# Weights of a two-layer hybrid model laid out contiguously, one 8 KB piece for each partition

## The reference, cut to what matters

```
h = x                                             # 256 tokens x 1024, float32
h = h + swa_sink_attention(rms_norm(h), a_w_qkv, a_b_qkv, a_sinks, a_w_o)
h = h + swiglu(rms_norm(h), f_w_gate, f_w_up, f_w_down)           # 1024 x 3584
h = h + gated_deltanet(rms_norm(h), b_w_in, b_conv_w, ..., b_w_o) # b_w_in 1024 x 4112
h = h + moe_swiglu(rms_norm(h), m_w_router, m_w_gate, m_w_up, m_w_down)  # 8 experts, top 2
return rms_norm(h)

def swiglu(h, w_gate, w_up, w_down):
    return (silu(h @ w_gate) * (h @ w_up)) @ w_down
```

## Time and profile before

| | |
|---|---|
| median of 3 runs | 1816.75 us (1814.03 to 1817.48) |
| span of the profiled execution | 1815.9 us, 0.85 below the median of the runs |
| TensorE busy | 1656.2 us, 91% |
| VectorE, ScalarE busy | 1285.9 us (71%), 1010.4 us (56%) |
| read from HBM | 431.73 MB, 238 GB/s over the span |
| mean granted clock of TensorE | 0.937 |

### The profile page before, as it was taken

One profiled execution on the slowest core, in us unless ns is written; L12 is line 12 of the kernel. 1 busy time (PEld: TensorE's weight loads), 2 busy tenths in 40 slices (PEclk: granted clock), 3 DMA queues, 4 the chain that ended last, 5 costly groups with the idle time before them and its releaser, 6 DMA issues.

```text
span 1815.9 us, 22294 instructions
## 1 busy us (share of the span) xinstructions
PE 1656.2 (91%) x8075; PEld 1380.0 (76%) x8075; DVE 1285.9 (71%) x1111; ACT 1010.4 (56%) x979; POOL 44.8 (2%) x42
## 2 busy tenths in 40 slices
PE   5889999979948587889999999999999999999996
PEld 4677888869838474778878878788788788788785
DVE  5735555548462433478898888888888888988885
ACT  3444334335421112267777767777777777777674
POOL 0000000000022020000000000000000000000000
PEclk9889999989968685889999999999999999999998
DMA  9214555535300000359999899899899899899992
GB/s 339 93 47 162 186 185 184 188 120 181 117 0 1 0 1 29 111 196 375 354 325 373 319 340 375 306 366 377 298 370 369 304 373 355 315 366 335 346 371 92
DMA packets 187186, 433.29 MB, mean 239 GB/s; under 512 B 9232, under 2 KB 9616, under 8 KB 187024
## 3 DMA queue, kind: packets, MB, share of 16 engines
q1 hardware_dynamic: 184032, 431.25, 66.1%
q10 hardware_dynamic: 3120, 1.56, 0.3%
HBM read 431.73 MB, written 1.05 MB: 238 GB/s over the span
## 4 chain that ended last, share of the span: by engine, by line
PE 81%; DVE 8%; ACT 6%; issue 3%; ACTq 1%; POOL 1%; DVEq 1%; POOLq 0%
PE PS L264 23%; PE PS L266 23%; PE PS L265 23%; ACT w_high L252 2%; DVE w_low L256 2%; PE PS L972 1%; PE PS L897 1%; PE PS L926 1%; PE PS L956 1%; PE PS L665 1%; PE PS L955 1%; PE PS L888 1%; PE PS L896 1%; ACT x_high L597 1%; PE PS L925 1%
## 5 line engine op out<-in xcount | busy, mean ns | idle before, releaser
L256 DVE TENSOR_TENSOR w_low<-w_raw,w_high 128x2048 fp32r<-128x2048 f32 x408 | 931.0, 2290 | 205.4 <-ACT w_high L252 203.4
L252 ACT ACTIVATE w_high<-w_raw 128x2048 fp32r<-128x2048 f32 x408 | 780.5, 1918 | 379.7 <-PE PS L266 378.7
L264 PE MATMUL PS<-w_high,x_high 128*128 128x512 f32 x1264 | 504.1, 399 | 23.1 <-DVE w_low L256 11.9
L266 PE MATMUL PS<-w_high,x_low 128*128 128x512 f32 x1264 | 495.2, 392 | 0.0
L265 PE MATMUL PS<-w_low,x_high 128*128 128x512 f32 x1264 | 494.9, 392 | 0.0
L264 PEld LDWEIGHTS PS<-w_high,x_high 128*128 128x128 f32 x1264 | 239.0, 189 | 82.1 <-DVE w_low L256 28.2
L266 PEld LDWEIGHTS PS<-w_high,x_low 128*128 128x128 f32 x1264 | 238.5, 189 | 51.2
L265 PEld LDWEIGHTS PS<-w_low,x_high 128*128 128x128 f32 x1264 | 238.9, 189 | 47.6
L264 PE MATMUL PS<-w_high,m_act_high 128*128 128x512 f32 x448 | 177.8, 397 | 0.0
L265 PE MATMUL PS<-w_low,m_act_high 128*128 128x512 f32 x448 | 177.3, 396 | 0.0
L266 PE MATMUL PS<-w_high,m_act_low 128*128 128x512 f32 x448 | 177.3, 396 | 0.0
(11 more groups left out here) (245 smaller groups left out, 1626.8 us busy)
## 6 DMA issues: line engine op xcount, KB each, us to landing
w_raw<-in_m_w_gate SPq DMA_DIRECT2D x112, 1024.0 KB, 6.9
w_raw<-in_m_w_up SPq DMA_DIRECT2D x112, 1024.0 KB, 6.9
w_raw<-in_m_w_down SPq DMA_DIRECT2D x112, 1024.0 KB, 6.4
w_raw<-in_b_w_in SPq DMA_DIRECT2D x16, 1024.0 KB, 5.5
w_raw<-in_f_w_gate SPq DMA_DIRECT2D x14, 1024.0 KB, 5.1
w_raw<-in_f_w_up SPq DMA_DIRECT2D x14, 1024.0 KB, 5.1
w_raw<-in_f_w_down SPq DMA_DIRECT2D x14, 1024.0 KB, 4.9
w_raw<-in_a_w_qkv SPq DMA_DIRECT2D x6, 1024.0 KB, 15.9
```

What stands on the lines that cost most here:

```text
L252: nc.scalar.activation(WH[:, n % SPLIT, :], W[:, n % RAW, :], ACT.Copy).then_inc(hi_done, 1)
L256: nc.vector.tensor_tensor(WL[:, n % SPLIT, :], W[:, n % RAW, :], WH[:, n % SPLIT, :].bitcast(f32), ALU.subtract).then_inc(lo_done, 1)
L264: nc.tensor.matmul(o, sH, mH, start=first, stop=False)
L266: return nc.tensor.matmul(o, sL, mH, start=False, stop=last)
```

## The change

The host cuts all large weights into blocks in the order in which SyncE reads them, each stored as 128 rows of 8 KB, one for each partition. Four arrays `w_att`, `w_ffn`, `w_gdn` and `w_moe` take the place of nine weight inputs, and `b_w_small` is the 16 columns of `b_w_in` that `small_w` takes. Every block then is one contiguous 1 MB in HBM. Slots, waits, order and the rest of the kernel stay as they are.

```diff
-        def fetch(sp, n, r, kind, src):
+        def fetch(sp, n, r, src):
             if n >= RAW:
                 sp.wait_ge(lo_done, n - RAW + 1 + r * RAW)
-            sp.dma_start(raw_view(n % RAW, kind), src).then_inc(w_in[n % RAW], 16)
+            sp.dma_start(W[:, n % RAW, :], src).then_inc(w_in[n % RAW], 16)
...
-        def col_src(w, cb, half):
-            return w.rearrange("(k p) c -> p k c", p=128)[:, 4 * half:4 * half + 4, cb * CH:(cb + 1) * CH]
...
+            def fetch_packed(n, w, first, last):
+                for i in range(first, last):
+                    fetch(sp, n + i, 0, w[i])
+
+            def ffn_stream(n0, r0, w, loop_r):
+
+                for i in range(4):
+                    fetch(sp, n0 + i, r0, w[i])
                 with sp.Fori(0, NC - 1) as i:
                     r = loop_r(i)
-                    for k, (w, half) in enumerate(((g, 0), (g, 1), (u, 0), (u, 1))):
-                        fetch(sp, n0 + 4 + k, r, "cols", block_of(w, half, i + 1))
-                    for half in range(2):
-                        fetch(sp, n0 + 8 + half, r, "rows", d[:, ds(4 * i + 2 * half, 2), :])
+                    for k in range(6):
+                        fetch(sp, n0 + 4 + k, r, w[ds(6 * i + 4 + k, 1)].rearrange("a p c -> p (a c)"))
...
             if "att" in stages:
-                fetch_cols(base["att"], a_w_qkv[0], 2)
+                fetch_packed(base["att"], w_att, 0, 4)
                 sp.dma_start(cst[:, 128:], consts[:, 128:]).then_inc(sem("cst_in"), 16)
-                fetch(sp, base["att"] + 4, 0, "cols", col_src(a_w_qkv[0], 2, 0))
-                fetch(sp, base["att"] + 5, 0, "cols", col_src(a_w_qkv[0], 2, 1))
-                fetch_cols(base["att"] + 6, a_w_o[0], D // CH)
+                fetch_packed(base["att"], w_att, 4, 10)
...
-                             (small_w[:, :, 0:16], b_w_in[0].rearrange("(k p) c -> p k c", p=128)[:, :, 4096:4112]),
+                             (small_w[:, :, 0:16], b_w_small.rearrange("(k p) c -> p k c", p=128)),
...
+def column_blocks(w):
+    n = w.shape[0]
+    c = w.shape[2] // CH
+    v = w.reshape(n, 2, 4, 128, c, CH).transpose(0, 4, 1, 3, 2, 5)
+    return v.reshape(n, c, 2, 128, SUB)
+
+
+def row_blocks(w):
+    n = w.shape[0]
+    return w.reshape(n, NC, 2, 2, 128, D).transpose(0, 1, 2, 4, 3, 5).reshape(n, NC, 2, 128, SUB)
```

More of the change, by code:

```diff
@@ L75, in constants, with hybrid_kernel @@
     return c
-def hybrid_kernel(nc, x, a_norm, a_w_qkv, a_b_qkv, a_sinks, a_w_o, f_norm, f_w_gate, f_w_up, f_w_down,
-                  b_norm, b_w_in, b_conv_w, b_a_log, b_dt_bias, b_o_norm, b_w_o,
-                  m_norm, m_w_router, m_w_gate, m_w_up, m_w_down, final_norm, consts, out,
+def hybrid_kernel(nc, x, a_norm, a_b_qkv, a_sinks, f_norm, b_norm, b_w_small, b_conv_w, b_a_log, b_dt_bias,
+                  b_o_norm, m_norm, m_w_router, final_norm, w_att, w_ffn, w_gdn, w_moe, consts, out,
                   stages=("att", "ffn", "gdn", "moe")):
@@ L275, in _ @@
         def _(sp):
-            def fetch_cols(n, w, blocks):
-                for cb in range(blocks):
-                    for half in range(2):
[L279 to L294, removed]
+            def fetch_packed(n, w, first, last):
[4 more added lines that the diff above has]
+                    fetch(sp, n0 + i, r0, w[i])
                 with sp.Fori(0, NC - 1) as i:
                     r = loop_r(i)
-                    for k, (w, half) in enumerate(((g, 0), (g, 1), (u, 0), (u, 1))):
-                        fetch(sp, n0 + 4 + k, r, "cols", block_of(w, half, i + 1))
-                    for half in range(2):
-                        fetch(sp, n0 + 8 + half, r, "rows", d[:, ds(4 * i + 2 * half, 2), :])
+                    for k in range(6):
+                        fetch(sp, n0 + 4 + k, r, w[ds(6 * i + 4 + k, 1)].rearrange("a p c -> p (a c)"))
                 for half in range(2):
-                    fetch(sp, n0 + SUBS_FFN - 2 + half, r0, "rows", d[:, 4 * (NC - 1) + 2 * half:4 * (NC - 1) + 2 * half + 2, :])
+                    fetch(sp, n0 + SUBS_FFN - 2 + half, r0, w[SUBS_FFN - 2 + half])
             x_v = x[0].rearrange("(t p) d -> p t d", p=128)
@@ L308, in _ @@
             if "att" in stages:
-                fetch_cols(base["att"], a_w_qkv[0], 2)
+                fetch_packed(base["att"], w_att, 0, 4)
                 sp.dma_start(cst[:, 128:], consts[:, 128:]).then_inc(sem("cst_in"), 16)
-                fetch(sp, base["att"] + 4, 0, "cols", col_src(a_w_qkv[0], 2, 0))
-                fetch(sp, base["att"] + 5, 0, "cols", col_src(a_w_qkv[0], 2, 1))
-                fetch_cols(base["att"] + 6, a_w_o[0], D // CH)
+                fetch_packed(base["att"], w_att, 4, 10)
             if "ffn" in stages:
-                ffn_stream(base["ffn"], 0, f_w_gate, f_w_up, f_w_down, lambda i: i)
+                ffn_stream(base["ffn"], 0, w_ffn, lambda i: i)
             if "gdn" in stages:
-                fetch_cols(base["gdn"], b_w_in[0], 8)
-                fetch_cols(base["gdn"] + 16, b_w_o[0], D // CH)
+                fetch_packed(base["gdn"], w_gdn, 0, 20)
             if "moe" in stages:
                 def job(j, e):
-                    ffn_stream(base["moe"], j * NC, m_w_gate[0, ds(e, 1)], m_w_up[0, ds(e, 1)], m_w_down[0, ds(e, 1)],
-                               lambda i: j * NC + i)
+                    n0, r0 = base["moe"], j * NC
+                    w = w_moe[ds(e, 1)].rearrange("a n p c -> (a n) p c")
+                    for i in range(4):
+                        fetch(sp, n0 + i, r0, w[i])
+                    with sp.Fori(0, NC - 1) as i:
+                        for k in range(6):
+                            fetch(sp, n0 + 4 + k, r0 + i, w[ds(6 * i + 4 + k, 1)].rearrange("a p c -> p (a c)"))
+                    for half in range(2):
+                        fetch(sp, n0 + SUBS_FFN - 2 + half, r0, w[SUBS_FFN - 2 + half])
                 with sp.Fori(0, E) as j:
@@ L1527, in _, with ffn_order @@
                                        op0=ALU.mult, op1=ALU.mult).then_inc(sem("fin_done"), 1)
-_INS = ['x', 'a_norm', 'a_w_qkv', 'a_b_qkv', 'a_sinks', 'a_w_o', 'f_norm', 'f_w_gate', 'f_w_up', 'f_w_down',
-        'b_norm', 'b_w_in', 'b_conv_w', 'b_a_log', 'b_dt_bias', 'b_o_norm', 'b_w_o',
-        'm_norm', 'm_w_router', 'm_w_gate', 'm_w_up', 'm_w_down', 'final_norm']
+_INS = ['x', 'a_norm', 'a_b_qkv', 'a_sinks', 'f_norm', 'b_norm', 'b_w_small', 'b_conv_w', 'b_a_log', 'b_dt_bias',
+        'b_o_norm', 'm_norm', 'm_w_router', 'final_norm', 'w_att', 'w_ffn', 'w_gdn', 'w_moe']
+def column_blocks(w):
[6 more added lines that the diff above has]
+    return w.reshape(n, NC, 2, 2, 128, D).transpose(0, 1, 2, 4, 3, 5).reshape(n, NC, 2, 128, SUB)
+def ffn_order(gate, up, down):
+    g, u, d = column_blocks(gate), column_blocks(up), row_blocks(down)
+    out = np.empty((gate.shape[0], SUBS_FFN, 128, SUB), np.float32)
+    out[:, 0:2], out[:, 2:4] = g[:, 0], u[:, 0]
+    for i in range(NC - 1):
+        n = 4 + 6 * i
+        out[:, n:n + 2], out[:, n + 2:n + 4], out[:, n + 4:n + 6] = g[:, i + 1], u[:, i + 1], d[:, i]
+    out[:, SUBS_FFN - 2:] = d[:, NC - 1]
+    return out
 def kernel(**inputs):
@@ L1539, with blocks @@
     nc = _bacc.Bacc("TRN2", target_bir_lowering=False, num_devices=1)
+    laid = {k: np.asarray(v) for k, v in inputs.items()}
+    def blocks(name, columns):
+        return column_blocks(laid[name][:, :, 0:columns]).reshape(-1, 128, SUB)
+    laid["w_att"] = np.concatenate([blocks("a_w_qkv", QKV), blocks("a_w_o", D)])
+    laid["w_gdn"] = np.concatenate([blocks("b_w_in", 4 * D), blocks("b_w_o", D)])
+    laid["b_w_small"] = laid["b_w_in"][0, :, 4 * D:]
+    laid["w_ffn"] = ffn_order(laid["f_w_gate"], laid["f_w_up"], laid["f_w_down"])[0]
+    laid["w_moe"] = ffn_order(laid["m_w_gate"][0], laid["m_w_up"][0], laid["m_w_down"][0])
     arrays, args = {}, []
     for name in _INS:
-        a = np.ascontiguousarray(inputs[name])
+        a = np.ascontiguousarray(laid[name])
         arrays[f"in_{name}"] = a
```

## The result

The changed kernel takes 1829.3 us in the median of four runs (1828.5 to 1830.0); the kernel before, run beside it, 1816.3. The ratio is 1.0072, 95% interval 1.0058 to 1.0087: slower by 0.7%. The profiled execution has a span of 1827.8 us, 11.9 more than before, and its own time is 1829.57.

The account below looks back on a forecast made before the run. TensorE was taken to bound the expert jobs, and ScalarE's held DMA issues to sit on the opening's path. Terms 0 + 9.4 + 0 were given as +9.5 us, so 1826.2 us; range 1810 to 1831, likeliest case 1822 to 1830.

Parts of the forecast that it names:

- step 3: Opening, ScalarE's queue: rows come up sooner, up to 2 us gained; half taken, leaving +9.4 us.
- step 2: Opening: ScalarE's remaining 887 packets pair with SyncE's mostly 8 KB ones, freeing it at 24.0 us, not 13.59: +10.4 us.
- The bound: Expert jobs: TensorE busy 125.32 of 127 us, transfers behind compute; in the opening, ScalarE held at its own DMA issues.
- Step 1: SyncE's weight blocks: 128 packets and 16 closing ones instead of 528 or 272; SyncE no longer stalls, 0 on the path.
- Step 4: First sum of squares to first matmul: 9.36 us of compute, so the delay goes through whole and nothing swallows it.
- Step 5: Rest of the kernel: blocks land sooner without gain, copies not slowed; 0, ends -1 and +2 us.
- The limit of 1500 packets: Opening: a DMA issue goes through when about 1500 packets of its own queue are left, each queue separately.
- The total of both queues: Opening: packets left in SyncE's and ScalarE's queues together (3391 and 2908) hold ScalarE's issues; 1811.5 us, chance 0.12.
- my first rival: Opening: total backlog holds ScalarE, so fewer SyncE packets free it; 5.2 us gained, 1811.5 us, chance 0.12.
- the stall goes: Opening: ScalarE freed early, third block the next limit, landing about 15.4; 5.2 us gained, 1811.5 us, chance 0.12.

Follow-up runs that it names:

- e1: Changed kernel, but the ten attention blocks stored as four 2 KB runs per partition; 1818.95 us, ratio 1.0005 to the kernel before.
- e2: Changed kernel, but the ten attention blocks stored as two 4 KB runs per partition; 1824.99 us, ratio 1.0044 to the kernel before.
- e5: Kernel before, with the router's part of `small_w` issued by ScalarE after its sums of squares; 1818.43 us, ratio 0.9998.
- e10: Changed kernel with ScalarE issuing `bias` and `sinks` ahead of both parts of `small_w`; 1819.21 us, ratio 1.0007 to the kernel before.
- e4: Changed kernel with `small_w` as one array of 128 rows of 768 B; 1814.99 us, ratio 0.9990 to the kernel before.
- e6: Kernel before (old layout of the large weights) with `small_w` as one array of 128 rows of 768 B; 1816.64 us, ratio 0.9990.
- e7: Changed kernel, packed `small_w`, SyncE issuing all but ScalarE's five row loads, x turned after the first block's copy; 1804.97 us, ratio 0.9940 to the kernel before.
- e8: Changed kernel, packed `small_w`, SyncE issuing most small loads, x turned after the first block's copy, run again; 1806.22 us, ratio 0.9931 to the kernel before.

## Why the prediction was right

The forecast was 1826.2 us, 9.5 more; it is 1829.3, 13.0 more, between the medians. The path was right and the price 3.5 us low: 1.0 is step 3, 0.45 is step 2, 1.1 comes after the first matmul, where two traces of one kernel differ by more, and the last microsecond lies between spans and medians.

*The bound.* Right: a job is 127 us as before, no wait for a block appears in it, and e1 shows no effect of 398 repacked blocks, to within 0.19%.

*Step 1, SyncE's queue.* Right: 59616 packets to the unit, and no issue of SyncE's in the opening waits.

*Step 2, ScalarE's backlog.* The mechanism was right. The packets alternate one to one at 8 KB, and e1, e2 and the changed kernel order the hold by packet size: last issue at 14.1, 22.4 and 24.4 us for 2, 4 and 8 KB. My sum gave 24.0. It rested on two counts that were each a little off: ScalarE had to start 955 packets and not 1032, and at 8 us it had started only 141, where I left it with 145 at 7. That the two nearly cancel is luck. The three issues took 20.67 us together, against my some 19.

*Step 3, rows that come up sooner.* Wrong, and this is the term that was mis-sized: I took 1 us off for it, and there was nothing to take off. The rows came up a microsecond later than before. Without it the sum would have been +10.4, measured +10.85.

*Step 4, the delay goes through whole.* Right: 25.77 to 35.13 is 9.36 us, as 14.92 to 24.28 was. The router weights landed at 28.1 us (24.4 after their issue), well ahead of their use. What I didn't have is the stretch of matmuls at the 1.2 GHz level, 1.6 us in the profiled execution.

*Step 5, no contention.* Right: a copy takes 1918 ns and a remainder 2289, 1918 and 2290 before.

*The limit of 1500 packets.* Wrong as a number, even for the kernel before. I read four of its held issues; two more in the same trace don't fit. The router's part went through at 6.96 us with 1360 - 142 = 1218 left, and SyncE's fourth block, held for 3.83 us, at 7.56 with 2016 - 664 = 1352 left:

```profile
3.73 3.83 SPq L246 DMA_DIRECT2D w_raw<-in_a_w_qkv  x1
```

The other runs widen it: `bias` at 1468 (after), 1539 (e1), 1200 (e2) and 1246 (e5) left, the router's part at 1118 after the change and 1180 in e10. An issue is held by what its own queue still has ahead, and here it went through somewhere between 1100 and 1600 packets; what sets the number is open. That `bias` had 1490 left before and 1468 after, so that step 2 could use one number for both, is luck: at e2's 1200 it would have come some 5 us later (268 packets more, at 55 in a us). The total of both queues, my first rival, is excluded by e5 and by the changed kernel's own counts.

*The rival "the stall goes".* Its mechanism fell, and so did its price when other edits took the hold away: I had the third block at 15.4 us, it came at 16.5 in the new layout and 20.0 in the old (e4, e6), because a `bias` that is no longer held competes with the blocks. The sum had a slip as well: 4.75 MB at 385 GB/s from 2 us on is 14.3, not 15.4. That rival was priced some 3 to 5 us too favourably.

## What to carry to other kernels

A larger packet on one DMA queue is a longer turn for every small packet on another: here a load of small packets advanced by 168, 104 or 55 in a us beside packets of 2, 4 or 8 KB. Before the rows of a large stream are made longer, look for a load of many short runs that is in flight beside it, and give that load one run for each partition first. Look for waits of DMA at the issuing engine too, in the chain of the opening. An engine that computes pays for its own queue's backlog, so its loads belong in few packets, with those of many packets last, or on an engine that only issues. And a wait that is worth nothing to remove, since another limit lies just behind it, can still cost its full price when it is made longer, as the 10.85 us here did.

## What was not expected of the hardware

- Two queues alternate packet for packet at every size tried: 176 to 176 in a us beside 2 KB packets, 415 to 415 in 4 us beside 4 KB, 109 to 110 in 2 us beside 8 KB, 92 to 93 in 2 us beside 9728 B. The typical 9 to 17 descriptors at a turn, which the Trainium skill gives in "DMA: Bandwidth & Descriptors", section "Queues, rings and completion order", appear in none of these stretches.
- The issue of one DMA held ScalarE for 13.58 us. The Trainium skill's "DMA: Bandwidth & Descriptors", section "Issuing engines are not separate DMA queues", calls the sequencer's time to start a DMA usually small relative to the DMA; here it was 13.58 us for a transfer that landed 18.7 us after its issue began.
- The first matmuls after a long idle opening ran 0.43 us apart for 3.6 us in one execution, and 0.23 apart from the start in another with the same opening. The lower rate is the 1.2 GHz level, as e5's record of 0.50 shows. A granted clock of 1.00 in a window ahead of a trace's first clock record (38.95 us after the change) shows nothing. Why the rise came at 13.54 us in e7 and at 18.46 in e8, which are the same kernel, is open.
